# Two transformer blocks on one core: the four parts of the split weights set 32 bytes apart

## What is computed

```python
mod  = silu(c) @ ada_w + ada_b                  # 1024 x 6144
proj = h @ w_in                                 # 1024 x 3584
x    = x + gate1 * (mixed @ w_out)              # 1024 x 1024
qry  = h2 @ w_query                             # 1024 x 2048
u    = expert_down[ids]; a = einsum(x, u)       # table 16384 x 1024
x    = x + gate2 * einsum(gelu(a) * gate, expert_up[ids])
z    = h @ w_in_2                               # 1024 x 2840
x    = x + mixed @ w_o_2                        # 1024 x 1024
x    = x + square(relu(h @ w_up_2)) @ w_down_2  # 1024 x 4096, 4096 x 1024
```

## Time and profile before

| what | value |
|---|---|
| median of 3 runs | 1400.43 us (1399.54 to 1402.03) |
| the profiled execution | 1399.0 us, its span 1397.2 us |
| PE busy | 1306.1 us, 93% of the span |
| PE weight loads busy | 1153.1 us, 83% |
| DVE busy | 988.3 us, 71% |
| ACT busy | 663.8 us, 48% |
| POOL busy | 289.4 us, 21% |
| granted TensorE clock | 0.966 on average |

### The profile page before, as it was taken

One profiled execution on the slowest core, in us unless ns is written; L12 is line 12 of the kernel. 1 busy time (PEld: TensorE's weight loads), 2 busy tenths in 40 slices (PEclk: granted clock), 3 DMA queues, 4 the chain that ended last, 5 costly groups with the idle time before them and its releaser, 6 DMA issues.

```text
span 1397.2 us, 20094 instructions
## 1 busy us (share of the span) xinstructions
PE 1306.1 (93%) x8122; PEld 1153.1 (83%) x8122; DVE 988.3 (71%) x1890; ACT 663.8 (48%) x868; POOL 289.4 (21%) x162
## 2 busy tenths in 40 slices
PE   3688988899999999999999999999999997899998
PEld 2566856799999999999988888888877686798987
DVE  5889844788999989954567676766775556565554
ACT  1445323345555555444544545554445464454543
POOL 0005000008887667772000000000000013000000
PEclk8798999999999999999999999999998998999999
DMA  9763634787877786886997887978654523355552
GB/s 345 263 238 123 214 121 148 265 300 221 257 234 235 241 268 175 253 295 237 362 316 280 287 286 270 309 278 303 241 203 148 187 78 147 108 185 192 181 183 89
DMA packets 141574, 316.61 MB, mean 227 GB/s; under 512 B 24347, under 2 KB 70684, under 8 KB 135850
## 3 DMA queue, kind: packets, MB, share of 16 engines
q1 hardware_dynamic: 104778, 264.92, 53.2%
q10 hardware_dynamic: 14016, 33.56, 6.4%
q0 software_dynamic: 22688, 16.86, 6.4%
HBM read 280.11 MB, written 35.20 MB: 226 GB/s over the span
## 4 chain that ended last, share of the span: by engine, by line
PE 81%; DVE 13%; DMA 2%; ACT 2%; issue 1%; SPq 1%; DVEq 0%; ACTq 0%
PE ps L662 11%; PE ps L661 10%; PE ps L663 10%; PE ps L649 10%; PE ps L650 10%; PE ps L651 10%; PE ps L627 3%; PE ps L629 3%; PE ps L628 3%; DVE w_lo L1567 3%; DVE peer_arena L1938 2%; DMA arena<-in_ada_w 2%; DVE peer_arena L1937 2%; PE ps L606 1%; DVE pages L1649 1%
## 5 line engine op out<-in xcount | busy, mean ns | idle before, releaser
L1567 DVE TENSOR_TENSOR w_lo<-wring,w_hi 128x1024 fp32r<-128x1024 f32 (+1 forms) x404 | 490.4, 1221 | 242.4 <-ACT w_hi L1150 238.0
L1150 ACT CAST w_hi<-wring 128x1024 fp32r<-128x1024 f32 (+1 forms) x404 | 420.8, 1045 | 341.9 <-PE ps L651 209.2
L649 PE MATMUL ps<-hT_hi,w_hi 128*128 128x256 f32 x1376 | 384.3, 279 | 5.7 <-DVE hT_lo L1592 5.3
L650 PE MATMUL ps<-hT_lo,w_hi 128*128 128x256 f32 x1376 | 382.2, 278 | 0.0
L651 PE MATMUL ps<-hT_hi,w_lo 128*128 128x256 f32 x1376 | 382.2, 278 | 0.0
L1519 POOL DMA_INDIRECT gates_of_second<-late x128 | 244.6, 1911 | 135.9 <-DVEq L1873 58.2
L649 PEld LDWEIGHTS ps<-hT_hi,w_hi 128*128 128x128 f32 x1376 | 259.3, 188 | 7.4 <-DVE hT_lo L1592 5.5
L651 PEld LDWEIGHTS ps<-hT_hi,w_lo 128*128 128x128 f32 x1376 | 260.1, 189 | 0.0
L650 PEld LDWEIGHTS ps<-hT_lo,w_hi 128*128 128x128 f32 x1376 | 259.1, 188 | 0.3
L662 PE MATMUL ps<-w_lo,a_hi 128*128 128x512 f32 x640 | 252.0, 394 | 0.0
L661 PE MATMUL ps<-w_hi,a_hi 128*128 128x512 f32 x640 | 250.5, 391 | 0.0
(11 more groups left out here) (307 smaller groups left out, 1346.4 us busy)
## 6 DMA issues: line engine op xcount, KB each, us to landing
wring<-in_peer_down SPq DMA_DIRECT2D x32, 2048.0 KB, 8.5
wring<-in_peer_up SPq DMA_DIRECT2D x32, 2048.0 KB, 7.9
wring<-in_w_in SPq DMA_DIRECT2D x12, 2048.0 KB, 8.6
pages<-in_ada_w POOLq DMA_DIRECT2D x8, 2048.0 KB, 8.5
acts_by_expert<-pages ACTq DMA_DIRECT2D x32, 512.0 KB, 4.1
peer_arena<-acts_by_expert SPq DMA_DIRECT2D x32, 512.0 KB, 8.8
wring<-in_w_up SPq DMA_DIRECT2D x8, 2048.0 KB, 8.7
wring<-in_w_down SPq DMA_DIRECT2D x8, 2048.0 KB, 7.8
```

Source lines behind the costliest of these rows:

```text
L649: pe.matmul(o, hi[:, k, :], hT_hi[:, k, :], start=(k == 0), stop=False)
L650: pe.matmul(o, hi[:, k, :], hT_lo[:, k, :], start=False, stop=False)
L1150: act.copy(split_part(kind, w_hi, u, width(kind, j)), part_of(kind, wring[:, n % RING, :], u, width(kind, j))).then_inc(split_hi, 1)
L1567: dve.tensor_tensor(lo, part_of(kind, wring[:, n % RING, :], u, width(kind, j)), hi, ALU.subtract)\
```

## The change

```diff
+APART = 8
...
-        w_hi = sb("w_hi", [P, PARTS, PART], F32R)
-        w_lo = sb("w_lo", [P, PARTS, PART], F32R)
+        w_hi = sb("w_hi", [P, PARTS, PART + APART], F32R)[:, :, 0:PART]
+        w_lo = sb("w_lo", [P, PARTS, PART + APART], F32R)[:, :, 0:PART]
```

## The result

The changed kernel took 1415.66 us (median of 4 runs, 1414.97 to 1417.01), the kernel before 1399.99 us beside it (median of 4). The ratio is 1.0104, with a 95% interval of 1.0083 to 1.0124: slower by 1%, outside the range given and on the side that had 18% of the chance. The profiled execution is the longest of the four; its span is 1415.2 us, 18.0 us more than before.

A forecast was written before the change was run, and what follows sets the result against it. PE's own pace was taken to bound the kernel. Terms of 0 for order, ACT and PE and 0 +- 0.3 us for DVE left the profiled execution at 1399.0 us; predicted median 1400.4 us, range 1395.5 to 1407 (0.88).

The forecast's parts named there:

- What bounds the kernel: Whole kernel: PE, busy 93% of the span, sets the end; only a change of its own pace moves it.
- DVE and ACT at 0: Subtractions into w_lo (DVE) and casts into w_hi (ACT): new remainders cost 0, DVE within 0.3 us either way.
- Between engines at 0: ACT, DVE and PE working on different parts at once: their traffic does not slow PE, 0.
- PE with itself at 0: PE's weight load beside the previous matmul: new address distances cost 0, bounds 4.4 ns up, 6.6 and 15.3 down per matmul.
- two readings: PE's pace in the trace before: equal at multiples of 512 bytes, and changing at 1248.92 us within one part at unchanged remainders.
- the surplus over 106.7 and 213.3 ns: PE's faster pace exceeds one column a cycle by 6.6 ns at 256 columns and 15.3 ns at 512.
- its own test: PE's matmuls: a clash of weight load against moving read would grow with the loads, not with the columns moved.
- The upper bound of 4.4 ns: PE's matmuls: the most that new distances were taken to add to each one.
- The range left out both clashes: PE's split matmuls: clash appears, 1420 us, chance 0.07; clash goes away, 1350 us, chance 0.05; neither in the range.
- the clash in the skewed parts: PE, three parts of four: load hits moving read, 4.4 ns per matmul, 20 us slower, 1420 us; chance 0.07.
- the choice of pace settling worse: PE in `row_part`, 691 to 1043 us: 1536 matmuls take the slower pace, 7.2 us, 1407.6 us; chance 0.11.
- The pace falls differently: PE's long stretches settle in the other pace: 1395.7 us if better, chance 0.10; 1407.6 us if worse, chance 0.11.

The follow-up runs named there:

- e4_ring32: Kernel before with wring moved by 32 bytes and w_hi, w_lo, a_hi, a_lo by 512: 1404.46 us against 1404.34, ratio 1.0009.
- f4_d192: Kernel before with w_hi and w_lo both moved 128 bytes against hT and a, one common distance of 192: 1426.38 us, ratio 1.0180.
- g2_a64: Kernel before with only a_hi, a_lo and arena moved, by 64 bytes: 1409.40 us against 1402.71, ratio 1.0055.
- f3_a256: Kernel before with only a_hi, a_lo and arena moved, by 256 bytes: 1401.17 us, ratio 1.0010.
- the last two experiments: Kernel before with w_lo 128 bytes later, a_hi, a_lo, arena 256, no skew: 1399.78 us; the same with a_lo another 128 later: 1401.07 us.
- h1_bases_again: Kernel before with w_lo 128 bytes later and a_hi, a_lo, arena 256, no skew, measured a second time: 1399.78 us against 1402.08, ratio 0.9983.
- g1_pair64: Kernel before with w_lo and a_lo both starting 128 bytes later, the rest at its remainder: 1403.29 us against 1402.71, ratio 1.0010.

## Why the prediction was wrong

*What bounds the kernel* held: PE's pace set the end. Busy time rose by 16.1 us on PE and by 0.2 us at most on DVE and ACT.

*DVE and ACT at 0* held, by the changed kernel's own rows and by e4_ring32.

*Between engines at 0* held as far as it was tried: e4_ring32 moves what ACT and DVE read against everything else and changes no pace.

*PE with itself at 0* is the step that failed. It rested on two readings. The first, that multiples of 512 bytes make no difference, was true and empty: every product of the kernel before stood at one and the same distance of 64. The trace of before held no information on others, and I said so, but then took the value 0 from an argument. The argument was that the surplus over 106.7 and 213.3 ns grows with the columns moved while loads don't. That speaks of the surplus, most of which indeed stays at every distance (226.7 ns is the best of all). It says nothing on what is added at another distance. The step of 4.4 to 4.7 ns between the two paces, which the prediction had measured too, is the same with 256 and with 512 columns: a cost per matmul, and so per load, as its own test asked of a clash. The test was put to the surplus and not to the step. The second reading, that the pace at 1248.92 us changed at unchanged addresses, was read as speaking against addresses. Its 123 ns are those of the first three matmuls behind the other loop, and neither of the two paces. f4_d192 turns it round: the slower pace, 117.8 and 233.3 ns, is the steady one at 192 bytes. At 64 both occur; with w_hi at 64 and w_lo at 192 only the faster did in the long stretches of the 256-column loop, in six traces. The upper bound of 4.4 ns was too low as well: a steady distance of 32 costs 5.0 ns, part 3 of the changed kernel 7.8.

*The rival that came true* was the clash in the skewed parts, with 0.07, at 20 us. The pace depends on the part, as its sign said, and the loss lies in PE alone; that it is the weight load that meets the moving read is not shown. Its price was a little high. In the 256-column loop parts 0 to 3 lost 0.8, 4.6, 4.7 and 7.8 ns against 113.3 (mean 4.5, for the 3.3 that three parts of four at 4.4 ns make), but in the 512-column loop the mean loss was 1.8 ns, since part 2 (384 for w_hi, 0 for w_lo) lost none. The three stages show 15.2 us. The range left out both clashes, though no row spoke on distances other than 64. (The prediction's own price for the choice of pace settling worse, 1407.6 us, also lay just above the 1407 at which its range ends.)

*The pace falls differently* is real too, though not what happened here: traces at a distance of 64 show the slower pace from 604 us on (before), in the first loop (g2_a64) or in the feed-forward part (f3_a256). Whether one kernel changes its choice from run to run isn't shown, as each of these has one trace. The kernel before ran from 1394.23 to 1410.05 us in 22 runs on one chip, and much of that follows the mean granted clock (0.970 in the fastest, 0.961 in the slowest). Something is left beside it: on the chip of the last two experiments seven runs of the kernel before at a clock of 0.963 lie between 1397.63 and 1403.02 us, while seven of h1_bases_again at 0.964 lie between 1399.09 and 1400.67. Three runs within 2.5 us had looked like more certainty than they were.

*The Trainium skill* (SBUF — State Buffer, Who interferes with whom) has PE's two read ports independent. The measured pace depends on the distance between what they read, by 5.0 ns on 113.3 at a steady distance and by up to 8 ns in a skewed part; here the measurement decides.

## What to carry to other kernels

When matmuls with their weight loads set the time, the remainder by 256 bytes between the stationary block being loaded and the moving block being read is worth a few runs: it changed the whole by up to 1.8% here, with no instruction touched. Give all parts of a buffer the same remainder, and read the pace as the count of matmuls in a window of a trace, which shows 1.5 ns where the time of a whole run, moved by the clock, doesn't. A trace in which every product stands at one distance says nothing on the others. And when a pace takes two values at the same work, ask of the step between them, too, what it grows with.

## What the runs showed of the hardware that was not expected

The distance from one matmul's start to the next, at a granted clock of 1.00 (2.4 GHz), took only a few steady values: 113.3, 117.8 and 118.3 ns with 256 columns of float32r, 226.7, 228.9, 230.4, 231.1 and 233.3 ns with 512. The distance between PE's stationary and moving operands, which fits a period of 256 bytes, picks among them; at 64 bytes two occur, and the one in force holds until a pause or other work of PE. Shifting both operands together by 32 bytes changed no pace (1591, 512 and 1225 matmuls in the three windows, as before). And a loop that ends a few microseconds earlier need not bring the kernel's end forward: the stage behind it took 190.1 us in e4_ring32 and 199.9 us in g1_pair64, in kernels that differ by gaps of some bytes.
